# Other buffers for the late routing tables, and one wait less ahead of the fifth expert's weights

## The reference, cut to what matters

```python
scores = jax.nn.sigmoid((t @ router_w).astype(jnp.float32))
sel = (scores + router_b.astype(jnp.float32)).reshape(-1, N_EXPERT_GROUPS, EXPERTS_PER_GROUP)
group_score = lax.top_k(sel, TOP_K)[0].sum(-1)
...
gates = jnp.sum(jax.nn.one_hot(ids, N_EXPERTS, dtype=jnp.float32) * w[..., None], axis=1).astype(h.dtype)
hid = jax.nn.silu(jnp.einsum('nd,edf->nef', t, w_gate)) * jnp.einsum('nd,edf->nef', t, w_up)
y = jnp.einsum('nef,efd->nd', hid * gates[:, :, None], w_down)
```

## Time and profile before

| | us |
|---|---|
| median of the runs (983.4, 985.73, 985.17) | 985.17 |
| the profiled execution | 980.98 |
| its span | 979.2 |
| TensorE busy in the span | 915.7 (94%) |
| VectorE busy | 493.7 (50%) |
| ScalarE busy | 181.8 (19%) |
| GpSimd busy | 161.6 (16%) |

### The profile page before, as it was taken

The page is one execution under the profiler, slowest core; times in us unless marked ns, Lnnn a source line. Parts: engine busy times, 40 slices in busy tenths (PEclk is TensorE's granted clock), DMA queues, the critical chain, the costliest instruction groups (busy, mean ns, idle before and its releaser), DMA issues.

```text
span 979.2 us, 11628 instructions
## 1 busy us (share of the span) xinstructions
PE 915.7 (94%) x4348; PEld 436.3 (45%) x4348; DVE 493.7 (50%) x1037; ACT 181.8 (19%) x386; POOL 161.6 (16%) x162
## 2 busy tenths in 40 slices
PE   3989999988899989999997999999999989999997
PEld 2423345755545545443442443433645545434432
DVE  1471574167456757333335752872446767433336
ACT  5210100266311111111112511101211111111100
POOL 4030361057400001000004200110000001000013
PEclk9999999989999989999999999999999989999999
DMA  9986945581520168999988453544250167999967
GB/s 346 396 331 261 342 185 188 162 230 51 179 113 22 44 278 322 412 420 414 421 331 299 170 209 121 222 173 172 67 225 22 44 279 268 408 423 421 421 272 300
DMA packets 71279, 243.97 MB, mean 249 GB/s; under 512 B 7617, under 2 KB 22753, under 8 KB 53809
## 3 DMA queue, kind: packets, MB, share of 16 engines
q1 hardware_dynamic: 44912, 201.12, 52.5%
q0 software_dynamic: 8528, 27.99, 7.7%
q10 hardware_dynamic: 17776, 14.04, 4.6%
HBM read 215.01 MB, written 27.33 MB: 247 GB/s over the span
## 4 chain that ended last, share of the span: by engine, by line
PE 83%; DMA 6%; DVE 5%; issue 2%; ACT 2%; POOL 1%; SPq 1%; DVEq 0%; ACTq 0%; POOLq 0%
PE bank L2278 15%; PE bank L2142 14%; PE bank L2130 14%; PE bank L2292 8%; PE bank L2111 7%; PE bank L2054 4%; PE bank L2068 4%; PE bank L2269 2%; PE bank L2181 2%; DMA ring<-in_moe_w_up 2%; DMA bz<-in_ada_w 2%; PE bank L2434 1%; DVE x_res L1437 1%; DMA ring<-in_ada_w 1%; PE bank L2581 1%
## 5 line engine op out<-in xcount | busy, mean ns | idle before, releaser
L2142 PE MATMUL bank<-ring,h_feat 128*128 128x512 f32 x320 | 145.3, 599 | 0.0
L2278 PE MATMUL bank<-ring,uv 128*32 128x512 f32 (+2 forms) x592 | 142.2, 596 | 3.1 <-ACT uv L1118 2.4
L2142 PEld LDWEIGHTS bank<-ring,h_feat 128*128 128x128 f32 x320 | 58.0, 190 | 59.8 <-issue 59.7
L2278 PEld LDWEIGHTS bank<-ring,uv 128*32 128x32 f32 (+2 forms) x592 | 45.9, 128 | 70.3 <-issue 66.0
L1683 DVE TENSOR_TENSOR uv<-uv,bank 128x256 f32<-128x256 f32 x25 | 10.5, 421 | 127.8 <-ACT uv L1126 127.8
L2292 PE MATMUL bank<-ring,uv 128*32 128x512 f32 (+2 forms) x296 | 72.7, 596 | 1.2 <-issue 0.6
L2111 PE MATMUL bank<-ring,h_feat 128*128 128x512 f32 x144 | 65.3, 609 | 2.7 <-issue 2.7
L2130 PE MATMUL bank<-ring,h_feat 128*128 128x512 f32 x144 | 64.1, 597 | 0.0
L982 POOL TENSOR_SCALAR h_tok<-h_tok 128x384 f32<-128x384 f32 (+1 forms) x40 | 44.1, 1115 | 61.4 <-DVE h_tok L1936 61.4
L1006 POOL DMA_INDIRECT uv<-h_rows,small x23 | 21.8, 948 | 193.2 <-PE bank L2269 158.3
L2278 PE MATMUL bank<-bz,uv 128*64 128x512 f32 (+1 forms) x112 | 49.4, 594 | 0.0
(11 more groups left out here) (321 smaller groups left out, 1380.1 us busy)
## 6 DMA issues: line engine op xcount, KB each, us to landing
bz<-in_ada_w SPq DMA_DIRECT2D x12, 2048.0 KB, 7.4
ring<-in_moe_w_gate SPq DMA_DIRECT2D x20, 1024.0 KB, 11.5
ring<-in_moe_w_up SPq DMA_DIRECT2D x20, 1024.0 KB, 13.5
ring<-in_moe_w_down SPq DMA_DIRECT2D x20, 1024.0 KB, 15.0
h_tok<-in_moe_w_down SPq DMA_DIRECT2D x12, 1024.0 KB, 15.4
y_rows<-uv SPq DMA_DIRECT2D x23, 512.0 KB, 14.5
ring<-in_ada_w SPq DMA_DIRECT2D x4, 2048.0 KB, 10.4
y_rows<-uv ACTq DMA_DIRECT2D x1, 6656.0 KB, 25.5
```

What stands on the lines that cost most here:

```text
L2142: last = mm(jbank(key)[:, :], HT[:, cc, P * t:P * (t + 1)], blk_ap(("out", layer, b))[:, cc, :], start=cc == 0, stop=cc == DC - 1)
L2278: last = mm(bank[2][32 * q:32 * (q + n), :], XT[:, b, cc, 32 * q:32 * (q + n)], w[:, :, cc, :], start=cc == 0, stop=cc == DC - 1)
```

## The change

It does two things. The working buffers of the late routing tables are no longer in `BZ[:, 2048:6144]`: the small ones go to `HTr[:, 4096:5120]`, two large ones to `PS` and `late_oh` to `Hr` from column 4736. The wait for `late_idx_mm` ahead of expert 4's loads is gone. The waits for `logits_done` and `h2_stored` stand before expert 3's loads, as before (`FIXED` is 3).

```diff
--- before.py
+++ after.py
@@ -482,16 +482,16 @@
         prod2, pos2 = routing(2 * E).rearrange("p (k e) -> p k e", k=2), routing(2)
 
 
-        ov_at = [2048]
+        ov_at = [4096]
 
         def late(n):
             ov_at[0] += n
-            assert ov_at[0] <= 6144
-            return BZ[:, ov_at[0] - n:ov_at[0]]
-
-        late_place = late(2 * TT * P).rearrange("p (k n) -> p k n", n=P)
-        late_tiles = late(2 * TT * NTILE).rearrange("p (k n) -> p k n", n=NTILE)
-        late_oh = late(2 * TT * (NTILE + MAXOV)).rearrange("p (k n) -> p k n", n=NTILE + MAXOV)
+            assert ov_at[0] <= 5120
+            return HTr[:, ov_at[0] - n:ov_at[0]]
+
+        late_place = PS[:, 1024:1024 + 2 * TT * P].rearrange("p (k n) -> p k n", n=P)
+        late_tiles = PS[:, 2304:2304 + 2 * TT * NTILE].rearrange("p (k n) -> p k n", n=NTILE)
+        late_oh = Hr[:, 4736:4736 + 2 * TT * (NTILE + MAXOV)].rearrange("p (k n) -> p k n", n=NTILE + MAXOV)
         ovf, inc, one16, delta = late(E), late(E), late(E), late(E)
         big, rowno, prod = [late(TT * E).rearrange("p (t e) -> p t e", e=E) for _ in range(3)]
         sl, hi, lo, wsum = late(2 * TT), late(2 * TT), late(2 * TT), late(TT)
@@ -813,11 +813,9 @@
                 sp.wait_ge(ids_ready, 2 * layer + 1)
                 for p in range(FIXED, WSLOTS):
                     ex = ranked_expert(p)
-                    if p == 3:
+                    if p == FIXED:
                         sp.wait_ge(logits_done, TT * (layer + 1))
                         sp.wait_ge(h2_stored, 16 * TT * (layer + 1))
-                    if p == 4:
-                        sp.wait_ge(late_idx_mm, layer + 1)
                     load_gate_up(layer, ex, p)
                     load_down(layer, ex, p)
```

## The result

| | before | changed |
|---|---|---|
| median, runs on one chip | 982.68 us (20 runs) | 986.43 us (20 runs) |
| ratio of the two, 95% interval | | 1.0041 [1.0029, 1.0052] |
| profiled execution, its span | 980.98 us, 979.2 us | 987.44 us, 985.6 us |

The change makes the kernel slower by 0.41%, some 4.0 us [2.8 to 5.1]. The forecast was no change that can be told, -0.5 us. 986.43 us lies in the range that was given, but that is luck: the 985.17 us on which the prediction built is the median of the first three of these 20 runs, and the median of all 20 is 982.68 us. What counts is the ratio, and its sign was missed.

What follows compares the result with a forecast made beforehand. TensorE, busy 94% of the span, was taken to set the time, with the DMA queue full beside it. -0.7 + 0.2 = -0.5 us gave 984.7 us; 8 in 10: 982.6 to 988.6 us.

Steps and rivals of the forecast that it cites:

- Term 1: Layer 1's expert stage: earlier loads remove TensorE's 0.69 us wait for a weight load; -0.7 us.
- Term 2: Pass 2's gather, both layers: takes 10.4 us beside early loads and g_b, stalling TensorE 0.15 and 0.06 us; +0.2 us.
- rival 1: TensorE's transposes for pass 2, each layer: gather over 12.1 us comes late; most likely +3.9 us, 989.1 us; chance 0.15.
- middle case: Pass 2's gather taking 12 us in both layers: +2.7 us, still within what can't be told.
- own range of the forecast: Whole kernel: 983.3 to 987.1 us, from -1.9 us to +1.9 us with gathers of 11.6 us; chance 0.73.
- Rival 2: Load queue in both layers: 1.3 and 2.0 us of backlog reach TensorE in full; -3.3 us, 981.9 us; chance 0.07.
- rival 3: Pass 2's gather lets SP's whole 5 MB pass, landing at 16.6 us; +12 us, 997 us; chance 0.02.
- rival 4: SP's queue: another wait holds SP, so the loads do not move; time stays 985.2 us; chance 0.03.
- The rule of the Trainium skill: Pass 2's gather meets one load and one broadcast more than when quiet: 8.4 us, sum -0.7 us.
- over 5 us later: Sign that the forecast is wrong: g_b lands over 5 us later than in the kernel before.
- Buffers at zero: Late routing arithmetic on VectorE: instructions and shapes stay, other buffer addresses cost nothing; 0 us.

Runs made afterwards that it cites:

- changed again: The changed kernel measured once more, with no edit: ratio 1.0043 [1.0026, 1.0061] to the kernel before.
- expert 5 waits: Changed kernel, but expert 5's gate and up loads wait for the late sums, so 3 MB instead of 5 MB come early: ratio 1.0043 [1.0027, 1.0058].
- early in layer 1: Changed kernel with the old wait put back for layer 0 only, so loads are early in layer 1 alone: ratio 1.0014 [0.999, 1.0037].
- gather 1.25 us late: Kernel before, with POOL issuing pass 2's gather behind that of pass 3, loads and broadcasts unmoved: ratio 1.0031 [1.0017, 1.0044].
- gather 2.5 us late: Kernel before, with POOL issuing pass 2's gather behind those of passes 3 and 4, loads and broadcasts unmoved: ratio 1.0072 [1.005, 1.0094].
- early broadcasts: Both g_b broadcasts issued before the expert stage: on the changed kernel 0.9999, then 1.001; on the kernel before 1.0009.

## Why the prediction was wrong

Price of one late gather, from the intervals (each less 13.98 us, less the wait). The wait that the profile lists is in every row 0.17 us shorter than the delay of the transposes' start, so the last column holds these 0.17 us too:

| version, layer | wait us | interval us | low clock us |
|---|---|---|---|
| changed, 1 | 1.24 | 17.00 | 1.8 |
| changed again, 1 | 1.13 | 16.92 | 1.8 |
| expert 5 waits, 0 and 1 | 0.59, 1.06 | 16.45, 16.91 | 1.9, 1.9 |
| early in layer 1 | 1.57 | 17.14 | 1.6 |
| gather 1.25 us late, 0 | 0.43 | 16.31 | 1.9 |
| gather 2.5 us late, 0 and 1 | 2.12, 2.13 | 18.96, 19.23 | 2.9, 3.1 |

- **Term 1, -0.7 us: right.** The changed kernel's trace runs 7.22 us behind that of before at pass 3's transposes of layer 1 (848.50 and 841.28 us) and 6.45 us behind at the products of the earlier trace rows, which begin at 912.43 us. The 0.8 us between hold the 0.69 us that were named.
- **Term 2, +0.2 us: the step that failed.** It measured 3.2 to 5.5 us: 3.0 us in layer 1 and 0.2 or 2.5 us in layer 0. The prediction took 10.4 us for the gather with all three sharers, out of 10.3 to 11.2, "because layer 1's gather had g_b beside it all along and landed in 8.6". With SP's queue full throughout and g_b beside it, the eight gathers that the profiles show took 11.0 to 12.0 us. The row that I leant on was of a gather that had g_b beside it, but SP's queue ran dry in its middle: it could not say what three full queues do. The estimate's upper end, 11.2 us, was nearest. Its lower end holds a slip: g_b is two broadcasts of 512 KB (the x2 above), and I counted the bytes of one. Both are 1 MB, 2.5 us at 417 GB/s, and 9.0 + 2.5 = 11.5 us, by the same estimate, is in the middle of what was measured (though only the first half had landed when the gather did, 10.5 us after its issue in layer 0, the second 15.2). From issue to use there are 10.25 and 10.34 us, so the waits are 0.6 to 1.6 us instead of 0.15 and 0.06 where TensorE comes on time.
- **The low clock was put in the wrong place.** The prediction knew the price (1.2 us as estimated; 1.6 to 1.9 measured) but charged it only in rival 1, beyond a gather of 12.1 us, and left it out of the middle case, "a gather of 12 us, costs 1.75 + 1.66 - 0.7 = +2.7 us". It came already behind a wait of 0.43 us. Priced so, the middle case is (1.57 + 1.6) x 2 - 0.7 = +5.6 us, and the own range of the forecast, which went to gathers of 11.6 us, would have held +4 us.
- **The sum as measured.** Layer 1: +3.0 us. Layer 0: 0.2 us where a low clock comes ahead of the sums, 2.5 us where it doesn't. Less 0.7: +2.5 to +4.8 us, around the measured 4.0.
- **Rival 1** named place and mechanism, with 0.15; this is what happened, with a shorter wait than it asked for. "None of 23 gathers took over 9.8 us" was no evidence against it, since none of the 23 ran under the new conditions.
- **Rival 2, rival 3, rival 4: fell.** The DMA share rose to 1.03 and 1.01 in the two stretches, and TensorE gained 0.7 us from it; no gather of pass 2 took over 12.0 us, where this rival needed 16.6; the loads did move.
- **The rule of the Trainium skill** gave a gather of 8.4 us and a sum of -0.7 us by my estimate. The rule stands (less depth changed nothing); the count that I hung on it was too low by some 3 us, of which the broadcast left out is 1.3.
- **g_b.** Expected to land at 389 to 391 us. VectorE waited 1.16 us for it in layer 0 and 0.34 in layer 1 (below), so it landed at 394.8 us in this execution, which runs 3.8 us behind the other there: at 391.0 on the prediction's scale. The second half took 15.2 and 16.2 us from its issue where it took 10.1 and 9.2 before. In layer 1 that is 7 us more, so the sign "over 5 us later" came true there; yet TensorE waited for nothing that follows.

```profile
394.84 1.23 DVE L1435 TENSOR_TENSOR bz<-bz 128x1024 f32<-128x1024 f32 x1 [1.16 <-DMA bz<-mod]
```

- **Buffers at zero: right,** by the version that loads behind the gather, measured twice.
- **The profiles alone mislead here.** 987.44 - 980.98 = 6.5 us, but 2.9 us of that are there before the first expert stage of layer 0 begins, in a part that the change doesn't touch, with other stretches of low clock. The 4.0 us are the ratio's.

Open: in layer 0 the changed kernel shows in both of its profiles a low clock that sets in between 375 and 378 us, ahead of the late sums. It costs 0.7 us there and hides the wait for the gather when it comes. The kernel before, the same with early broadcasts, the version early in layer 1, the one with expert 5 waiting and the one with the gather 2.5 us late show none there. The version with the loads behind the gather and that with the early broadcasts have it in one profile of two. But the version with the buffers alone and the kernel before with the gather behind one other have it too, and neither moves a load:

```profile
378.00:380.00 2.00, 1.59 (x10) 0.96 (x12) 1.29 (x7) 0.98 (x2) 1.29 (x2) 0.50 1.05 442
...
375.00:376.60 1.60, 1.41 (x7) 1.01 (x5) 0.81 (x3) 0.58 (x1) 0.95 (x1) 0.50 1.02 430
```

So it needs no early load, and none of its 0.7 us is charged to the change above. In 14 profiles it stands in 4 of the 6 with early loads in layer 0 and in 3 of the other 8; whether the change makes it more frequent wasn't settled.

## What to carry to other kernels

Before loads are moved forward, list the small transfers that somebody waits for in the time that will be filled, and give each the distance from its issue to its use: here 10.25 us, against 9.6 us at an incomplete load. Count every transfer that will run beside it, in bytes. Price the stall with the clock that falls behind it: on this kernel a wait of half a microsecond on TensorE cost 2.3 to 2.5 us. The gather grew by 1.5 us in layer 0 and by 3.0 to 3.4 us in layer 1, and margins of 0.65 and 1.7 us were both too small. If the loads must go early, let them start when the small transfer has landed, or take one of the other sharers away; both gave the time back here, and neither won more than can be measured.

## What the runs showed of the hardware

- A gather of 512 KB against its company: 4.5 to 5.4 us with quiet queues (pass 1's; the first loads are issued 1 to 1.5 us behind it), 9.2 to 9.8 us beside a full load queue (early broadcasts), 11.0 to 12.0 us beside a full load queue and the broadcasts. The second queue costs some 4.5 us, the third 2 us more. The gather's own queue adds up: those of passes 3 and 4, issued right behind, took 14.8 and 17.2 us in the changed kernel, where before none took over 9.8.
- In these rows the low clock's price behind a wait goes in steps and not with the wait's length: 1.6 to 1.9 us for six waits of 0.43 to 1.57 us, 2.9 and 3.1 us for two of 2.1 us. Next to the edge there is none: four times the transposes began 0.14 to 0.25 us late (both profiles of the changed kernel and the version early in layer 0, in layer 0; the gather 1.25 us late, in layer 1), the clock stayed at 1.00, and the interval was 14.16 to 14.26 us. The wait of 0.43 us, a start 0.6 us late, had it in full.
- The order of three gathers on POOL, with no byte added, was worth 7.1 us of 982 [4.9 to 9.2 us].
